# Dividing attention probabilities by their sums: in the transposing matmul instead of behind the values product

## The chip, the cores and the metric

The kernel runs on one core of a Trainium2 chip. TensorE multiplies and transposes and writes to PSUM, whose 8 banks hold 512 f32 columns each. VectorE, ScalarE and GpSimd do the rest, and each engine takes its instructions in program order, waiting on counting semaphores. The metric is device time in microseconds, lower is better.

## The reference, cut to what matters

One layer: RMSNorm, a combined projection, latent attention (8 heads) beside a gated MLP, then a mixture of experts and a last norm. The attention is, for 1024 rows in blocks of 128 queries:

```
sc = (einsum('bqhd,bkhd->bhqk', qn_i, k_nope)
      + einsum('bqhr,bkr->bhqk', qr_i, k_rope)).astype(float32) * scale
mask = key_chunk[None, :] <= q_chunk[:, None]        # chunks of 64 rows
p = softmax(where(mask, sc, neg), axis=-1)
o = einsum('bhqk,bkhd->bqhd', p, v)
```

So p is the exponentials divided by their row sums, and o is p times v. All of it is float32.

## The kernel before, in words

The stages follow each other in one program: norm and transposes, latents, attention ("A"), the gated MLP's projections ("U"), the gates and output products, the router, the experts. The sets of instructions of each engine are written out by hand, in the order in which they run. To keep float32 accuracy most products are done in three: each operand is split into a high part (`_hi`) and a rest (`_lo`), both of type fp32r, and `mm3` (L369 to L371) multiplies high by high, high by rest and rest by high. Transposes (`pe.transpose` with `ident`) and a few small products use plain f32.

Attention runs over 64 steps s, which are 8 heads h of 8 query blocks i. Block i sees i + 1 key tiles of 128. For each step:

- `scores(s)` on TensorE fills two PSUM banks with 128 queries by up to 1024 keys; `row_max(s)` on VectorE (L1274) takes the negative row maxima; `exponent(s)` on ScalarE (L987) writes the exponentials to `prob` and their row sums to `lsum`.
- `prob_transposes(s)` on TensorE (L658) turns each 128x128 tile of `prob`, four to a PSUM bank, in a pass; passes alternate between banks 4 and 5. ScalarE copies a pass to `pt_hi` (L1013) and VectorE takes the rest `pt_lo` (L1319).
- `values(s)` multiplies v by the turned tiles into bank 6, as 64 rows of one head by 128 queries. After four steps bank 6 is full, and ScalarE copies it to `o_t` (L979).

The row sums are taken care of once in four steps: `inverse_sums` on VectorE (L1280) makes four columns of reciprocals `rl`, `spread_sums` on TensorE (L667) turns each column, broadcast to 128 columns, so that bank 4 or 5 holds the reciprocal of each query in every partition, and `outputs` on VectorE (L1289) multiplies `o_t` by it. `PASSES` and `bank_of` give the spreads a place among the passes over banks 4 and 5.

TensorE's order in step s is `scores(s + 2)`, `prob_transposes(s)`, `values(s - 1)`, after every fourth step `spread_sums`, and in the first four steps of a head one `job` of the next head, which projects its queries or keys. VectorE's order is `row_max(s + 2)`, `pt_lo` of step s, `outputs`, `job_read`. ScalarE's is `exponent(s + 1)`, `pt_hi` of step s, `outputs`, `job_high`. `scores(s + 2)` waits until `exponent(s)` has read the banks that it fills.

Two plain f32 products that are no transposes stand outside attention: L574 multiplies squares by a column of ones, and L582 multiplies ones by the diagonal matrices `z_diag`. `link` makes VectorE wait for its own last instruction.

Of the kernel before, what the change touches and what calls it, by code (L numbers as in the profile page):

```python
# [20 lines left out]
F32 = mybir.dt.float32  # L21
# [4 lines left out]
ALU = mybir.AluOpType  # L26
ACT = mybir.ActivationFunctionType
AX = mybir.AxisListType.X

P = 128  # L30
# [4 lines left out]
HALF = 512  # L35
EPS = 1e-6
HEADS, NOPE, ROPE, VH = 8, 64, 32, 64
# [22 lines left out]
NQ = 64  # L60
# [17 lines left out]
def chunks_through(s):  # L78

    return sum((i % NT) // 4 + 1 for i in range(s + 1))  # L80

PASSES = []
for _s in range(NQ):
    PASSES += [(0, _c) for _c in range(chunks_through(_s - 1) if _s else 0, chunks_through(_s))]
    if _s % 4 == 0 and _s:
        PASSES.append((1, _s // 4 - 1))
PASSES.append((1, NQ // 4 - 1))  # L90
PASS_OF = {_x: _n for _n, _x in enumerate(PASSES)}


def build(nc, a, out, stop_after=None):
    base = 16512

    with ExitStack() as ctx:
        def at(name, kb, shape, dt):
            return nc.alloc_sbuf_tensor_at(name, shape, dt, offset=base + int(kb * KB))
# [3 lines left out]
        def sem(name):  # L103
            if name not in sems:
                sems[name] = ctx.enter_context(nc.semaphore(name))
            return sems[name]
# [64 lines left out]
        pt_hi = [at(f"pt_hi{i}", (20, 24, 36, 40)[i], [P, 4, P], F32R) for i in range(4)]  # L171
        pt_lo = [at(f"pt_lo{i}", (22, 26, 38, 42)[i], [P, 4, P], F32R) for i in range(4)]
        q_tmp = at("q_tmp", 6, [P, HALF], F32)
        q_hi = [at(f"q_hi{i}", 136 + 8 * i, [P, T], F32R) for i in range(2)]
        q_lo = [at(f"q_lo{i}", 140 + 8 * i, [P, T], F32R) for i in range(2)]
        v_hi = [at(f"v_hi{i}", 152 + 4 * i, [P, NT, VH], F32R) for i in range(2)]
# [224 lines left out]
        def head_values(h):  # L401

            p = h // 2
            return v_f[p // 2][:, (p % 2) * (p // 2 + 1), :, (h % 2) * VH:(h % 2 + 1) * VH]

        def bank_of(kind, n):
            return 4 + PASS_OF[kind, n] % 2

        def v_tiles_after(jj):

# [129 lines left out]
        def _(pe):  # L540
# [55 lines left out]
            if "A" in on:  # L596
# [44 lines left out]
                            mm = pe.matmul(dst[:, m - CHUNK:m], mask_l[:, :], mask_r[:, :], start=False, stop=True)  # L641
                    mm.then_inc(sem("s_done"), 1)

                def bank_free(kind, n):

                    if PASS_OF[kind, n] >= 2:
                        was, m = PASSES[PASS_OF[kind, n] - 2]
                        pe.wait_ge(sem("o_ready" if was else "pt_lo_ready"), m + 1)

                def prob_transposes(s):  # L650

                    i = s % NT
                    c0 = chunks_through(s - 1) if s else 0
                    pe.wait_ge(sem("exp_done"), s + 1)
                    for c in range(i // 4 + 1):
                        bank_free(0, c0 + c)
                        for j in range(4 * c, min(4 * c + 4, i + 1)):
                            mm = pe.transpose(ps[:, bank_of(0, c0 + c), (j % 4) * P:(j % 4) * P + P],  # L658
                                              prob[s % 2][:, j * P:(j + 1) * P], ident[:, :])
                        mm.then_inc(sem("pt_done"), 1)  # L660

                def spread_sums(g):

                    pe.wait_ge(sem("rl_ready"), g + 1)
                    bank_free(1, g)
                    for i in range(4):
                        mm = pe.transpose(ps[:, bank_of(1, g), i * P:(i + 1) * P],  # L667
                                          rl[:, 4 * g + i:4 * g + i + 1].to_broadcast([P, P]), ident[:, :])
                    mm.then_inc(sem("sums_spread"), 1)

                def values(s):

                    h, i = divmod(s, NT)
                    c0 = chunks_through(s - 1) if s else 0
                    pe.wait_ge(sem("v_split"), h + 1)
                    pe.wait_ge(sem("pt_lo_ready"), chunks_through(s))
                    if s and s % 4 == 0:
                        pe.wait_ge(sem("o_copied"), s // 4)
                    dst = ps[0:VH, 6, (i % 4) * P:(i % 4 + 1) * P]
                    for j in range(i + 1):  # L680
                        c = (c0 + j // 4) % 4
                        mm = mm3(pe, dst, (v_hi[h % 2][:, j, :], v_lo[h % 2][:, j, :]),
                                 (pt_hi[c][:, j % 4, :], pt_lo[c][:, j % 4, :]), j == 0, j == i)
                    mm.then_inc(sem("pv_done"), 1)
# [17 lines left out]
                for s in range(NQ):  # L702
                    if s + 2 < NQ:
                        scores(s + 2)
                    prob_transposes(s)
                    if s:
                        values(s - 1)
                        if s % 4 == 0:
                            spread_sums(s // 4 - 1)
                    h, i = divmod(s, NT)  # L710
                    if i < 4 and h + 1 < HEADS:
                        job(h + 1, i)
                values(NQ - 1)
                spread_sums(NQ // 4 - 1)
            if "U" in on:
                def v_rows(t):

# [195 lines left out]
        def _(act):  # L913
# [50 lines left out]
            if "A" in on:  # L964
# [9 lines left out]
                def outputs(g):  # L974

                    h, c = divmod(g, 2)
                    r = (h % 2) * VH
                    act.wait_ge(sem("pv_done"), 4 * g + 4)
                    act.activation(o_t[r:r + VH, h // 2, c * HALF:(c + 1) * HALF], ps[0:VH, 6, :], ACT.Copy).then_inc(sem("o_copied"), 1)  # L979

                def exponent(s):
                    n = (s % NT + 1) * P
# [17 lines left out]
                for s in range(NQ):  # L1000
                    h, i = divmod(s, NT)
                    if s + 1 < NQ:
                        exponent(s + 1)
                    c0 = chunks_through(s - 1) if s else 0
                    for c in range(i // 4 + 1):
                        w = min(4, i + 1 - 4 * c)
                        cc = c0 + c
                        act.wait_ge(sem("pt_done"), cc + 1)
                        if cc >= 4:

                            used = next(x for x in range(s + 1) if chunks_through(x) > cc - 4)
                            act.wait_ge(sem("pv_done"), used + 1)
                        act.activation(pt_hi[cc % 4][:, 0:w, :].rearrange("p a b -> p (a b)"), ps[:, bank_of(0, cc), 0:w * P],  # L1013
                                       ACT.Copy).then_inc(sem("pt_hi_ready"), 1)
                    if s % 4 == 0 and s:
                        outputs(s // 4 - 1)
                    if i < 4 and h + 1 < HEADS:
                        job_high(h + 1, i)
# [136 lines left out]
        def _(dve):  # L1155
            steps = [0]

            def link(ins):

                steps[0] += 1  # L1160
                ins.then_inc(sem("dve_step"), 1)
                dve.wait_ge(sem("dve_step"), steps[0])
# [95 lines left out]
            if "A" in on:  # L1258
# [15 lines left out]
                    dve.tensor_reduce(negm[:, s:s + 1], ps[:, b:b + 2, :].rearrange("p b c -> p (b c)")[:, 0:n], AX, ALU.max,  # L1274
                                      negate=True).then_inc(sem("max_ready"), 1)

                def inverse_sums(g):

                    dve.wait_ge(sem("exp_done"), 4 * g + 4)
                    dve.reciprocal(rl[:, 4 * g:4 * g + 4], lsum[:, 4 * g:4 * g + 4]).then_inc(sem("rl_ready"), 1)  # L1280

                def outputs(g):

                    h, c = divmod(g, 2)
                    r = (h % 2) * VH
                    o = o_t[r:r + VH, h // 2, c * HALF:(c + 1) * HALF]
                    dve.wait_ge(sem("o_copied"), g + 1)
                    dve.wait_ge(sem("sums_spread"), g + 1)
                    dve.tensor_tensor(o, ps[r:r + VH, bank_of(1, g), :], o, ALU.mult).then_inc(sem("o_ready"), 1)  # L1289

                for t in range(1, NT, 2):
                    dve.wait_ge(sem("v_done"), t + 1)
# [12 lines left out]
                    job_read(0, j)  # L1305
                row_max(0)
                row_max(1)
                for s in range(NQ):
                    h, i = divmod(s, NT)
                    if (s + 1) % 4 == 3:  # L1310
                        inverse_sums((s + 1) // 4)
                    if s + 2 < NQ:
                        row_max(s + 2)
                    c0 = chunks_through(s - 1) if s else 0
                    for c in range(i // 4 + 1):
                        w = min(4, i + 1 - 4 * c)
                        cc = c0 + c
                        dve.wait_ge(sem("pt_hi_ready"), cc + 1)
                        dve.tensor_tensor(pt_lo[cc % 4][:, 0:w, :].rearrange("p a b -> p (a b)"), ps[:, bank_of(0, cc), 0:w * P],  # L1319
                                          pt_hi[cc % 4][:, 0:w, :].rearrange("p a b -> p (a b)").bitcast(F32), ALU.subtract).then_inc(sem("pt_lo_ready"), 1)  # L1320
                    if s % 4 == 0 and s:
                        outputs(s // 4 - 1)
                    if i < 4 and h + 1 < HEADS:
                        job_read(h + 1, i)
                outputs(NQ // 4 - 1)
            if "O" in on:
                for k in range(KS):
                    dve.wait_ge(sem("ot_hi_ready"), k + 1)
# [408 lines left out]
```

## Time and profile before

| | |
|---|---|
| median of 3 runs | 1250.52 us (1250.46 to 1253.19) |
| the profiled execution | 1250.46 us, of which span 1248.4 us |
| TensorE busy | 1108.9 us, 89% of the span |
| VectorE, ScalarE, GpSimd busy | 712.3, 564.8, 327.0 us |
| granted clock, mean | 0.951 |
| attention, `job` of the first head to the last `spread_sums` | about 97 to 300 us |

Each row of the profile names a line of the kernel, the engine, and output<-inputs. TensorE's weight loads are an engine of their own in it (PEld), beside the matmuls (PE). A matmul's end is modelled: the distance from one start to the next tells more than its duration. An idle time is put down to the engine that ended it.

### The profile page before, as it was taken

The page shows a single profiled execution, that of the slowest core. Times are in us where ns is not written, and L with a number is a line of the kernel's source. Part 1 is how long each engine was busy: PE and PEld are TensorE (multiplying, and loading weights), DVE is VectorE, ACT ScalarE, POOL GpSimd, SP SyncE. Part 2 cuts the span into 40 slices and gives each one's busy share as a digit, 9 for nine tenths or more (in the row PEclk, how much of TensorE's full clock was granted, in tenths as well). Part 3 has the DMA queues.
Part 4 walks back from the last instruction along what each step waited for, and adds up shares of the span by engine and source line. Part 5 has one row for each costly group of instructions (what it writes and reads, how often), then busy time and mean ns, then how long its engine had stood idle before and what let it go on. Part 6 is the DMA issues. An engine that isn't in the chain of part 4 may idle for free.

```text
span 1248.4 us, 18136 instructions
## 1 busy us (share of the span) xinstructions
PE 1108.9 (89%) x6835; PEld 963.9 (77%) x6835; DVE 712.3 (57%) x832; ACT 564.8 (45%) x756; POOL 327.0 (26%) x276
## 2 busy tenths in 40 slices
PE   3998999999999899999998999329999999999940
PEld 3885888888877788888887888329999999999930
DVE  5874666666055711111114232558888888888838
ACT  5334655655144200000003221407888888888823
POOL 3103222212332223333220000122444444444210
PEclk9988999999999999999999999659999999999975
DMA  7010000021204111111113322537999999999737
GB/s 244 1 28 11 7 7 7 7 69 34 52 1 111 34 34 51 49 37 50 51 51 104 105 75 77 212 121 300 394 368 356 341 348 356 363 379 358 284 141 288
DMA packets 93131, 184.27 MB, mean 148 GB/s; under 512 B 29712, under 2 KB 67088, under 8 KB 79248
## 3 DMA queue, kind: packets, MB, share of 16 engines
q1 hardware_dynamic: 82704, 166.65, 38.4%
q0 software_dynamic: 10368, 16.80, 3.6%
q8 instruction: 41, 0.67, 0.2%
q14 instruction: 18, 0.15, 0.0%
HBM read 177.12 MB, written 27.26 MB: 164 GB/s over the span
## 4 chain that ended last, share of the span: by engine, by line
PE 78%; DVE 11%; ACT 4%; issue 2%; DMA 2%; SPq 1%; POOL 0%; ACTq 0%; POOLq 0%; DVEq 0%
PE ps L369 24%; PE ps L371 23%; PE ps L370 23%; PE ps L858 3%; PE ps L658 2%; DVE pt_lo L1319 1%; PE ps L818 1%; DVE negm L1274 1%; SPq L348 1%; DVE q_tmp L1265 1%; ACT prob L987 1%; DVE acc L1600 1%; DVE res L1610 1%; DVE acc L1601 1%; PE ps L667 1%
## 5 line engine op out<-in xcount | busy, mean ns | idle before, releaser
L1554 DVE TENSOR_TENSOR we_lo<-raw_e,we_hi 128x2048 fp32r<-128x2048 f32 x108 | 246.9, 2288 | 48.3 <-ACT we_hi L1096 48.3
L1096 ACT ACTIVATE we_hi<-raw_e 128x2048 fp32r<-128x2048 f32 x108 | 206.1, 1908 | 8.3 <-DMA raw_e<-in_w_exp_gate_dram 3.7
L369 PE MATMUL ps<-ht_hi,w_hi 128*128 128x512 f32 x448 | 176.4, 394 | 0.4 <-DVE ht_lo L1192 0.4
L371 PE MATMUL ps<-ht_hi,w_lo 128*128 128x512 f32 x448 | 174.7, 390 | 0.0
L370 PE MATMUL ps<-ht_lo,w_hi 128*128 128x512 f32 x448 | 174.6, 390 | 0.0
L369 PE MATMUL ps<-we_hi,xst_hi 128*128 128x256 f32 x576 | 169.4, 294 | 0.0
L370 PE MATMUL ps<-we_lo,xst_hi 128*128 128x256 f32 x576 | 163.5, 284 | 0.0
L371 PE MATMUL ps<-we_hi,xst_lo 128*128 128x256 f32 x576 | 163.4, 284 | 0.0
L363 POOL CAST w_hi<-raw 128x1024 fp32r<-128x1024 f32 x36 | 40.7, 1130 | 302.2 <-PE ps L371 270.3
L369 PEld LDWEIGHTS ps<-we_hi,xst_hi 128*128 128x128 f32 x576 | 111.4, 193 | 0.0
L370 PEld LDWEIGHTS ps<-we_lo,xst_hi 128*128 128x128 f32 x576 | 111.1, 193 | 0.0
L371 PEld LDWEIGHTS ps<-we_hi,xst_lo 128*128 128x128 f32 x576 | 110.9, 193 | 0.0
L1398 DVE TENSOR_TENSOR mix<-ps,mix 128x512 f32<-128x512 f32 x16 | 11.1, 691 | 167.6 <-PE ps L371 167.6
L369 PEld LDWEIGHTS ps<-ht_hi,w_hi 128*128 128x128 f32 x448 | 84.4, 188 | 18.1 <-issue 1.0
L371 PEld LDWEIGHTS ps<-ht_hi,w_lo 128*128 128x128 f32 x448 | 84.2, 188 | 17.7
L370 PEld LDWEIGHTS ps<-ht_lo,w_hi 128*128 128x128 f32 x448 | 84.4, 188 | 17.3 <-issue 0.2
L364 POOL TENSOR_TENSOR w_lo<-raw,w_hi 128x1024 fp32r<-128x1024 f32 x36 | 87.4, 2428 | 2.9
L1053 ACT ACTIVATE mix<-ps 128x512 f32<-128x512 f32 x16 | 8.7, 598 | 146.4 <-PE ps L371 146.4
L1674 POOL COPY xcol<-xidx 128x1 uint32 (+1 forms) x36 | 61.5, 1709 | 36.6 <-DVE xidx L1548 34.6
L369 PE MATMUL ps<-we_hi,hidt_hi 128*128 128x512 f32 x144 | 59.5, 413 | 4.8 <-DVE hidt_lo L1568 2.5
L1319 DVE TENSOR_TENSOR pt_lo<-ps,pt_hi 128x512 fp32r<-128x512 f32 (+2 forms) x96 | 50.5, 553 | 20.9 <-ACT pt_hi L1013 20.6
L1013 ACT ACTIVATE pt_hi<-ps 128x512 fp32r<-128x512 f32 (+2 forms) x96 | 43.5, 488 | 36.8 <-PE ps L658 36.8
(284 smaller groups left out, 2472.8 us busy)
## 6 DMA issues: line engine op xcount, KB each, us to landing
raw_e<-in_w_exp_gate_dram SPq DMA_DIRECT2D x36, 1024.0 KB, 8.6
raw_e<-in_w_exp_up_dram SPq DMA_DIRECT2D x36, 1024.0 KB, 7.9
raw_e<-in_w_exp_down_dram SPq DMA_DIRECT2D x36, 1024.0 KB, 8.7
raw<-in_w_in_dram SPq DMA_DIRECT2D x27, 512.0 KB, 3.8
yin<-y_dram SPq DMA_DIRECT2D x16, 512.0 KB, 6.6
xin<-in_x_dram SPq DMA_DIRECT2D x8, 512.0 KB, 7.2
raw<-in_w_out_dram SPq DMA_DIRECT2D x8, 512.0 KB, 4.1
xre<-in_x_dram SPq DMA_DIRECT2D x8, 512.0 KB, 4.2
```

Source lines behind the costliest of these rows:

```text
L363: pool_link(pool, pool.tensor_copy(w_hi[n % 3][:, :, :], raw[n % 3][:, :, :]))
L364: pool.tensor_tensor(w_lo[n % 3][:, :, :], raw[n % 3][:, :, :], w_hi[n % 3][:, :, :].bitcast(F32), ALU.subtract).then_inc(sem("w_split"), 1)
L369: pe.matmul(dst, st[0], mv[0], start=first, stop=False)
L370: pe.matmul(dst, st[0], mv[1], start=False, stop=False)
L371: return pe.matmul(dst, st[1], mv[0], start=False, stop=last)
L658: mm = pe.transpose(ps[:, bank_of(0, c0 + c), (j % 4) * P:(j % 4) * P + P], prob[s % 2][:, j * P:(j + 1) * P], ident[:, :])
L858: mm = pe.transpose(ps[:, k // 4, (k % 4) * P:(k % 4) * P + P], v[:, k, :], ident[:, :])
L1013: act.activation(pt_hi[cc % 4][:, 0:w, :].rearrange("p a b -> p (a b)"), ps[:, bank_of(0, cc), 0:w * P], ACT.Copy).then_inc(sem("pt_hi_rea ...
L1096: act.activation(we_hi[c % 4][:, :], raw_e[c % 6][:, :], ACT.Copy).then_inc(sem("w_hi_ready"), 1)
L1319: dve.tensor_tensor(pt_lo[cc % 4][:, 0:w, :].rearrange("p a b -> p (a b)"), ps[:, bank_of(0, cc), 0:w * P], pt_hi[cc % 4][:, 0:w, :].rearr ...
L1554: dve.tensor_tensor(we_lo[c % 4][:, :], raw_e[c % 6][:, :], we_hi[c % 4][:, :].bitcast(F32), ALU.subtract).then_inc(sem("w_lo_ready"), 1)
L1674: pool.tensor_copy(xcol[j % 4][:, :], xidx[:, column(it, j)]).then_inc(sem("xcol_ready"), 1)
```

## The change

The division moves from behind the values product into the transposing. On VectorE `diagonal(s)` takes the reciprocal of one column of row sums and multiplies the identity by it, to a 128x128 f32 tile `rl_diag` (two buffers). `prob_transposes(s)` multiplies each tile of `prob` by `rl_diag` in a plain f32 matmul where it transposed it with the identity, so that `pt_hi` and `pt_lo` hold probabilities that are already divided. It waits for `diag_ready` instead of `exp_done`. `inverse_sums`, `spread_sums` and VectorE's `outputs` go away, and with them the list of passes: banks 4 and 5 alternate over the chunks alone. ScalarE's copy to `o_t` is the last step.

```
-                    pe.wait_ge(sem("exp_done"), s + 1)
+                    pe.wait_ge(sem("diag_ready"), s + 1)
                     for c in range(i // 4 + 1):
-                        bank_free(0, c0 + c)
+                        if c0 + c >= 2:
+                            pe.wait_ge(sem("pt_lo_ready"), c0 + c - 1)
                         for j in range(4 * c, min(4 * c + 4, i + 1)):
-                            mm = pe.transpose(ps[:, bank_of(0, c0 + c), (j % 4) * P:(j % 4) * P + P],
-                                              prob[s % 2][:, j * P:(j + 1) * P], ident[:, :])
+                            mm = pe.matmul(ps[:, 4 + (c0 + c) % 2, (j % 4) * P:(j % 4) * P + P],
+                                           prob[s % 2][:, j * P:(j + 1) * P], rl_diag[s % 2][:, :], start=True, stop=True)
                         mm.then_inc(sem("pt_done"), 1)
-                def spread_sums(g):
...
-                        if s % 4 == 0:
-                            spread_sums(s // 4 - 1)
...
-                def inverse_sums(g):
...
-                def outputs(g):
...
-                    dve.tensor_tensor(o, ps[r:r + VH, bank_of(1, g), :], o, ALU.mult).then_inc(sem("o_ready"), 1)
+                def diagonal(s):
+
+                    dve.wait_ge(sem("exp_done"), s + 1)
+                    link(dve.reciprocal(rl[:, s:s + 1], lsum[:, s:s + 1]))
+                    if s >= 2:
+                        dve.wait_ge(sem("pt_done"), chunks_through(s - 2))
+                    dve.tensor_scalar(rl_diag[s % 2][:, :], ident[:, :], rl[:, s:s + 1], None, ALU.mult).then_inc(sem("diag_ready"), 1)
...
                 row_max(0)
                 row_max(1)
+                diagonal(0)
                 for s in range(NQ):
                     h, i = divmod(s, NT)
-                    if (s + 1) % 4 == 3:
-                        inverse_sums((s + 1) // 4)
+                    if s + 1 < NQ:
+                        diagonal(s + 1)
                     if s + 2 < NQ:
                         row_max(s + 2)
```

On TensorE, at the eighth block of the first head, before: scores with their mask (L641), then eight transposes with `ident`, then the values product.

```order
L369 MATMUL ps<-k_hi_141,q_hi_132 128x256
L370 MATMUL ps<-k_lo_143,q_hi_132 128x256
L371 MATMUL ps<-k_hi_141,q_lo_134 128x256
L641 MATMUL ps<-mask_r,mask_l 128x64
L658 MATMUL ps<-ident,prob_145 128x128 x8
L369 MATMUL ps<-pt_hi_122,v_hi_135 64x128
L370 MATMUL ps<-pt_lo_126,v_hi_135 64x128
```

The same place in the changed program, whose lines are numbered 10 to 18 lower:

```order
L359 MATMUL ps<-k_hi_143,q_hi_134 128x256
L360 MATMUL ps<-k_lo_145,q_hi_134 128x256
L361 MATMUL ps<-k_hi_143,q_lo_136 128x256
L628 MATMUL ps<-mask_r,mask_l 128x64
L640 MATMUL ps<-rl_diag_132,prob_147 128x128 x8
L359 MATMUL ps<-pt_hi_122,v_hi_137 64x128
L360 MATMUL ps<-pt_lo_126,v_hi_137 64x128
```

Only the operand has changed from `ident` to `rl_diag`, and the kind of the instruction from a transpose to a matmul.

On TensorE after the values product of the eighth block, before: four broadcast columns are turned (L667), then the next head's projection (`c_hi`, `h_hi`) starts.

```order
L369 MATMUL ps<-pt_hi_125,v_hi_135 64x128
L370 MATMUL ps<-pt_lo_129,v_hi_135 64x128
L371 MATMUL ps<-pt_hi_125,v_lo_137 64x128
L667 MATMUL ps<-ident,rl 128x128 x4
L369 MATMUL ps<-c_hi,h_hi_113 128x512
L370 MATMUL ps<-c_lo,h_hi_113 128x512
```

The same place in the changed program:

```order
L359 MATMUL ps<-pt_hi_125,v_hi_137 64x128
L360 MATMUL ps<-pt_lo_129,v_hi_137 64x128
L361 MATMUL ps<-pt_hi_125,v_lo_139 64x128
L359 MATMUL ps<-c_hi,h_hi_113 128x512
L360 MATMUL ps<-c_lo,h_hi_113 128x512
```

The turned columns are gone and nothing stands in their place.

On VectorE over the last three steps of the first head, before: `negm` is a row maximum, `pt_lo` the rest of a pass.

```order
L1274 TENSOR_REDUCE negm<-ps 128x1
L1319 TENSOR_TENSOR pt_lo_128<-ps,pt_hi_124 128x512
L1319 TENSOR_TENSOR pt_lo_129<-ps,pt_hi_125 128x256
L1280 RECIPROCAL rl<-lsum 128x4
L1274 TENSOR_REDUCE negm<-ps 128x1
L1319 TENSOR_TENSOR pt_lo_126<-ps,pt_hi_122 128x512
L1319 TENSOR_TENSOR pt_lo_127<-ps,pt_hi_123 128x384
L1274 TENSOR_REDUCE negm<-ps 128x1
L1319 TENSOR_TENSOR pt_lo_128<-ps,pt_hi_124 128x512
L1319 TENSOR_TENSOR pt_lo_129<-ps,pt_hi_125 128x512
```

The same steps in the changed program:

```order
L1250 RECIPROCAL rl<-lsum 128x1
L1253 TENSOR_SCALAR rl_diag_132<-ident,rl 128x128
L1244 TENSOR_REDUCE negm<-ps 128x1
L1284 TENSOR_TENSOR pt_lo_126<-ps,pt_hi_122 128x512
L1284 TENSOR_TENSOR pt_lo_127<-ps,pt_hi_123 128x384
L1250 RECIPROCAL rl<-lsum 128x1
L1253 TENSOR_SCALAR rl_diag_131<-ident,rl 128x128
L1244 TENSOR_REDUCE negm<-ps 128x1
L1284 TENSOR_TENSOR pt_lo_128<-ps,pt_hi_124 128x512
L1284 TENSOR_TENSOR pt_lo_129<-ps,pt_hi_125 128x512
L1250 RECIPROCAL rl<-lsum 128x1
L1253 TENSOR_SCALAR rl_diag_132<-ident,rl 128x128
```

A reciprocal of one column and a 128x128 product now stand ahead of each row maximum, behind the `pt_lo` of the step before.

## Rows read from the trace of the kernel before

**Rows 1.** The page: busy time and share; granted TensorE clock in 40 slices.
```profile
PE 1108.9 (89%) x6835; PEld 963.9 (77%) x6835; DVE 712.3 (57%) x832; ACT 564.8 (45%) x756; POOL 327.0 (26%) x276
...
PEclk9988999999999999999999999659999999999975
```

**Rows 2.** Busy time by engine: a middle head, and the last one.
```profile
184.30:208.80 24.50, 23.33 (x216) 20.28 (x215) 16.36 (x28) 14.65 (x34) 5.76 (x7) 1.00 0.04 8
...
282.00:301.00 19.00, 17.27 (x181) 15.67 (x180) 11.72 (x20) 11.17 (x23) 0.81 (x1) 1.00 0.01 2
```

**Rows 3.** TensorE groups, whole run: count, busy us, mean ns, idle before.
```profile
L658 PE MATMUL ps<-ident,prob 128*128 128x128 f32 x288 | 44.2, 280 | 1.3 <-DVE pt_lo L1319 1.0
...
L667 PE MATMUL ps<-ident,rl 128*128 128x128 f32 x64 | 9.9, 277 | 5.4 <-DVE pt_lo L1319 5.4
...
L574 PE MATMUL ps<-ones,c_sq 128*128 128x1 f32 x48 | 5.8, 254 | 0.0
...
L582 PE MATMUL ps<-z_diag,ones 128*128 128x512 f32 x8 | 4.2, 642 | 0.0
```

**Rows 4.** TensorE in order of time: start, us, line, shapes, count, idle before.
```profile
186.78 0.47 PE L369 MATMUL ps<-k_hi,q_hi 128*128 128x512 f32 x1 [0.31 <-ACT prob L987]
...
196.22 0.62 PE L667 MATMUL ps<-ident,rl 128*128 128x128 f32 x4 [0.68 <-DVE pt_lo L1319]
196.60 0.48 PE L369 MATMUL ps<-k_hi,q_hi 128*128 128x512 f32 x1
...
200.04 0.20 PE L641 MATMUL ps<-mask_r,mask_l 128*128 128x64 bf16 x1
200.42 0.96 PE L658 MATMUL ps<-ident,prob 128*128 128x128 f32 x7 [0.17 <-DVE pt_lo L1319]
...
202.73 1.07 PE L658 MATMUL ps<-ident,prob 128*128 128x128 f32 x8
203.56 0.30 PE L369 MATMUL ps<-pt_hi,v_hi 128*64 128x128 f32 x1
```

**Rows 5.** The same view where 128x512 f32 matmuls stand among split ones.
```profile
68.51 0.39 PE L371 MATMUL ps<-ht_hi,w_lo 128*128 128x512 f32 x1
68.74 1.88 PE L582 MATMUL ps<-z_diag,ones 128*128 128x512 f32 x4
...
70.68 0.40 PE L370 MATMUL ps<-ht_lo,w_hi 128*128 128x512 f32 x1
```

**Rows 6.** The same view where the 128x1 f32 matmuls stand.
```profile
56.01 1.84 PE L574 MATMUL ps<-ones,c_sq 128*128 128x1 f32 x16
...
58.03 0.40 PE L370 MATMUL ps<-ht_lo,w_hi 128*128 128x512 f32 x1
```

**Rows 7.** Weight loads of the four broadcasts: count, busy, mean, idle before.
```profile
L667 PEld LDWEIGHTS ps<-ident,rl 128*128 128x128 f32 x64 | 6.6, 136 | 6.3 <-issue 6.3
```

**Rows 8.** ScalarE early in a head, ahead of the fifth score block.
```profile
185.45 0.63 ACT L970 ACTIVATE q_hi<-q_tmp 128x512 fp32r<-128x512 f32 x1 [2.03 <-DVE q_tmp L1265]
...
185.99 0.56 ACT L987 ACTIVATE prob<-ps,negm 128x384 f32<-128x384 f32 x1
```

**Rows 9.** VectorE groups, whole run: reciprocals, scalar operation, the removed product.
```profile
L1289 DVE TENSOR_TENSOR o_t<-ps,o_t 64x512 f32<-64x512 f32 x16 | 11.0, 688 | 18.0 <-ACT o_t L979 12.6 <-PE ps L667 5.4
...
L1280 DVE RECIPROCAL rl<-lsum 128x4 f32<-128x4 f32 x16 | 2.8, 172 | 2.7 <-ACT prob L987 2.7
...
L1426 DVE RECIPROCAL rstd<-std 128x1 f32<-128x1 f32 x8 | 1.3, 164 | 13.6 <-ACT std L1082 13.6
...
L1165 DVE TENSOR_SCALAR ident<-iota_row,iota_col 128x128 f32<-128x128 f32 x1 | 0.3, 288 | 1.2 <-POOL iota_col L1618 1.2
```

**Rows 10.** VectorE groups in the attention stage, 95 to 301 us: the row maxima.
```profile
L1274 DVE TENSOR_REDUCE negm<-ps 128x1 f32<-128x128 f32 (+3 forms) x64 | 47.8, 748 | 14.7 <-PE ps L641 14.0
```

**Rows 11.** ScalarE groups there: exponentials and the reads of their sums.
```profile
L987 ACT ACTIVATE prob<-ps,negm 128x128 f32<-128x128 f32 (+3 forms) x64 | 47.0, 735 | 0.3
...
L987 ACT ACTIVATION_READ_ACCUMULATOR prob<-ps,negm 128x1 f32 x64 | 12.6, 198 | 0.0
```

More of the change, by code:

```diff
@@ L80, in chunks_through @@
     return sum((i % NT) // 4 + 1 for i in range(s + 1))
[L85 to L91, printed above, removed]
 def build(nc, a, out, stop_after=None):
@@ L173, in build @@
         q_tmp = at("q_tmp", 6, [P, HALF], F32)
+        rl_diag = [at(f"rl_diag{i}", 5 + i / 2, [P, P], F32) for i in range(2)]
         q_hi = [at(f"q_hi{i}", 136 + 8 * i, [P, T], F32R) for i in range(2)]
@@ L404, in head_values @@
             return v_f[p // 2][:, (p % 2) * (p // 2 + 1), :, (h % 2) * VH:(h % 2 + 1) * VH]
-        def bank_of(kind, n):
-            return 4 + PASS_OF[kind, n] % 2
         def v_tiles_after(jj):
@@ L642, in scores @@
                     mm.then_inc(sem("s_done"), 1)
[L644 to L648, printed above, removed]
                 def prob_transposes(s):
@@ L653, in prob_transposes @@
                     c0 = chunks_through(s - 1) if s else 0
-                    pe.wait_ge(sem("exp_done"), s + 1)
+                    pe.wait_ge(sem("diag_ready"), s + 1)
                     for c in range(i // 4 + 1):
-                        bank_free(0, c0 + c)
+                        if c0 + c >= 2:
+                            pe.wait_ge(sem("pt_lo_ready"), c0 + c - 1)
                         for j in range(4 * c, min(4 * c + 4, i + 1)):
-                            mm = pe.transpose(ps[:, bank_of(0, c0 + c), (j % 4) * P:(j % 4) * P + P],
-                                              prob[s % 2][:, j * P:(j + 1) * P], ident[:, :])
+                            mm = pe.matmul(ps[:, 4 + (c0 + c) % 2, (j % 4) * P:(j % 4) * P + P],
+                                           prob[s % 2][:, j * P:(j + 1) * P], rl_diag[s % 2][:, :], start=True, stop=True)
                         mm.then_inc(sem("pt_done"), 1)
-                def spread_sums(g):
[L664 to L669, printed above, removed]
                 def values(s):
@@ L677, in values @@
                     if s and s % 4 == 0:
-                        pe.wait_ge(sem("o_copied"), s // 4)
+                        pe.wait_ge(sem("o_ready"), s // 4)
                     dst = ps[0:VH, 6, (i % 4) * P:(i % 4 + 1) * P]
@@ L713, in _ @@
                 values(NQ - 1)
-                spread_sums(NQ // 4 - 1)
             if "U" in on:
@@ L978, in outputs @@
                     act.wait_ge(sem("pv_done"), 4 * g + 4)
-                    act.activation(o_t[r:r + VH, h // 2, c * HALF:(c + 1) * HALF], ps[0:VH, 6, :], ACT.Copy).then_inc(sem("o_copied"), 1)
+                    act.activation(o_t[r:r + VH, h // 2, c * HALF:(c + 1) * HALF], ps[0:VH, 6, :], ACT.Copy).then_inc(sem("o_ready"), 1)
                 def exponent(s):
@@ L1012, in _ @@
                             act.wait_ge(sem("pv_done"), used + 1)
-                        act.activation(pt_hi[cc % 4][:, 0:w, :].rearrange("p a b -> p (a b)"), ps[:, bank_of(0, cc), 0:w * P],
+                        act.activation(pt_hi[cc % 4][:, 0:w, :].rearrange("p a b -> p (a b)"), ps[:, 4 + cc % 2, 0:w * P],
                                        ACT.Copy).then_inc(sem("pt_hi_ready"), 1)
@@ L1275, in row_max @@
                                       negate=True).then_inc(sem("max_ready"), 1)
-                def inverse_sums(g):
-                    dve.wait_ge(sem("exp_done"), 4 * g + 4)
-                    dve.reciprocal(rl[:, 4 * g:4 * g + 4], lsum[:, 4 * g:4 * g + 4]).then_inc(sem("rl_ready"), 1)
-                def outputs(g):
[L1284 to L1288, printed above, removed]
-                    dve.tensor_tensor(o, ps[r:r + VH, bank_of(1, g), :], o, ALU.mult).then_inc(sem("o_ready"), 1)
+                def diagonal(s):
[4 more added lines that the diff above has]
+                    dve.tensor_scalar(rl_diag[s % 2][:, :], ident[:, :], rl[:, s:s + 1], None, ALU.mult).then_inc(sem("diag_ready"), 1)
                 for t in range(1, NT, 2):
@@ L1318, in _ @@
                         dve.wait_ge(sem("pt_hi_ready"), cc + 1)
-                        dve.tensor_tensor(pt_lo[cc % 4][:, 0:w, :].rearrange("p a b -> p (a b)"), ps[:, bank_of(0, cc), 0:w * P],
+                        dve.tensor_tensor(pt_lo[cc % 4][:, 0:w, :].rearrange("p a b -> p (a b)"), ps[:, 4 + cc % 2, 0:w * P],
                                           pt_hi[cc % 4][:, 0:w, :].rearrange("p a b -> p (a b)").bitcast(F32), ALU.subtract).then_inc(sem("pt_lo_ready"), 1)
-                    if s % 4 == 0 and s:
-                        outputs(s // 4 - 1)
                     if i < 4 and h + 1 < HEADS:
                         job_read(h + 1, i)
-                outputs(NQ // 4 - 1)
             if "O" in on:
```

## The prediction

> **What bounds the kernel now.** I read the page's first two parts first. TensorE is busy for 1108.9 us of the span of 1248.4 us, and its granted clock is at nine tenths or full in all slices but the first ones and two stretches far behind attention [rows 1]. The change touches attention alone, so the next view is the busy time in stretches. In a middle head of 24.5 us TensorE is busy for 23.33 us at the full clock (2.4 GHz), VectorE for 16.36 us and ScalarE for 14.65 us. The last head, which has no projections beside it, has TensorE busy for 17.27 of 19.0 us [rows 2]. TensorE's work sets the pace of a head, and the other two can only put holes into it. TensorE in order of time shows the holes: one before the fifth score block, where it waits for an exponential (idle 0.31 us), one before the turned sums (0.68 us), a small one before the seventh block's transposes (0.17 us) [rows 4]. So what the change does to TensorE's own time comes first, and what it does to these holes second.
>
> **The transposes become matmuls: the large term.** There are 288 of them, 36 tiles in each of 8 heads [rows 3]. Eight stand from 202.73 to 203.56 us, where the values product starts, which is 0.104 us for one [rows 4]; I take 0.107. What a plain f32 matmul of 128 columns takes, no row of attention shows. Two others do. L582 has 4 matmuls in the program (two in each of two calls) and 8 records in the trace; L574 has 24 and 48 records [rows 3]. One plain f32 matmul is two records, one transpose is one. Four records of L582, 512 columns each, stand between 68.74 us and the split product behind them. Split products of 512 columns start 0.23 us apart (68.51 to 68.74), so that the first one behind them started in effect at 70.68 - 0.23 = 70.45 us. That is 1.71 / 4 = 0.427 us for a record, and a quarter of it, 0.107 us, for 128 columns, if columns set it [rows 5]. L574 has one column, so that its records show the loading of weights alone: (58.03 - 0.23 - 56.01) / 16 = 0.112 us for a record [rows 6]. At 128 columns load and columns are about equal. Where they overlap, as under L582, a matmul costs 2 x 0.107 to 2 x 0.112 us, and the transpose before it 0.107. I take 0.11 us more for a tile: 288 x 0.11 = +31.7 us. The bounds: 288 x 0.107 = 30.8 and 288 x 0.117 = 33.7 where they overlap; nothing added if a record of this shape held all of it (against the two counts of rows 3); and if load and columns ran one after the other, 2 x (0.107 + 0.107) = 0.428 us, which is +0.321 us for a tile and +92.4 us in all. The nearest rows are the two of 0.107 and 0.112, and I stay with them.
>
> The Trainium skill, page "TensorE: Matmul & The Clock Gate", section Terms, calls trn2's transpose mode 4 times faster for FP32. If that held for a tile here, a matmul would take four times 0.107 us, and the time would come out as in the second rival below. The trace disagrees as far as it goes: two records of 0.107 us make a factor of two.
>
> **The turned sums go.** There were 16 groups of four. One takes 196.60 - 196.22 = 0.38 us [rows 4], so -6.1 us, all of it on TensorE's path. The wait in front of the groups goes with them. It comes in every second group, because the four columns need the bank whose last `pt_lo` VectorE has just finished: 5.4 us by the matmul rows [rows 3], 6.3 us by the rows of the weight loads, which don't have modelled ends [rows 7]. The score block or projection behind it needs nothing that is so late, so I count -6.3 us. VectorE also loses 16 products of 0.688 us and 16 reciprocals of 0.172 us, 13.8 us [rows 9]. They are not on the path and I cost them at nothing.
>
> **The diagonals on VectorE.** The nearest rows are a reciprocal of one column (0.164 us) and the building of the identity, 128x128 f32 with one scalar operand (0.288 us) [rows 9]. With a hop of 0.03 us between them a diagonal is 0.48 us, and 64 of them are 30.8 us. VectorE's load in a middle head goes from 16.36 to about 18.5 us (+3.9, -1.7), in a head that will last near 27. As work this is hidden. As order it isn't free. `diagonal(s + 1)` waits for the exponential of step s + 1, and `row_max(s + 2)`, the `pt_lo` of step s and `job_read` are queued behind it. Before, `row_max(s + 2)` waited only for its scores. The exponential after it, and TensorE two steps on, wait for that maximum.
>
> I followed one head through by these durations. Three places matter. At the second block the exponential of the third (185.99 us) stands behind `q_hi` on ScalarE [rows 8], and TensorE waits for it with its fifth score block [rows 4]. That chain starts at the projection in the first block, and the two tiles of the second block stand on TensorE between this projection and the hole, so their 2 x 0.11 us fall into it: 0.2 us in 7 heads, -1.5 us. At the third block the row maximum of the fourth now starts only after that exponential and its diagonal, about 1.8 us later than before, `pt_lo` and `k_lo` follow it, and the next projection waits for `k_lo` by about 0.15 us. At the seventh block the transposes wait for the `pt_lo` of the sixth, which now stands behind the diagonal as well as the long row maximum: the step from 200.04 to 200.42 us grows by about 0.1 us. With some more for what I can't follow, 0.3 us in each of 8 heads, +2.4 us. The bounds: -7 us, if the longer matmuls hide the rest of the holes (1.17 us of idle TensorE in a middle head [rows 2], less the 0.68 already counted and what stays for the projection chain, doubled for the seams that the rows don't count as idle), and +12 us as in the first rival.
>
> **The rest.** Passes over banks 4 and 5 now alternate without the sums between them. The wait that this leaves is for a `pt_lo` two passes back, as before. ScalarE's copy to `o_t` stays as it was. The end of attention has its last turned group removed, which is in the 16. The stages behind it start from TensorE's end of attention and only shift. Attention runs at full clock, so nothing is to be gained there. The cold stretch at its start contains one tile.
>
> **The sum.** 31.7 - 6.1 - 6.3 - 1.5 + 2.4 = +20.2 us. On the profiled execution, 1250.46 us (a span of 1248.4 and 2.1 around it), that is 1270.7 us. The median of the three runs, 1250.52, is the same within 0.1 us.
>
> **Rivals.**
> 1. VectorE and ScalarE become a second bound. Row maximum, exponential, reading of the sum and diagonal now form a chain from step to step. Over attention that is 47.8 [rows 10] + 47.0 + 12.6 [rows 11] + 30.8, and hops of about 0.15 us in each of 64 steps, 9.6: 148 us against some 225 us of attention. So it doesn't bind as a whole. Over the first blocks of a head, where TensorE's step is 2 us and `job_read` stands in the same queue, it can. If 1.5 us a head stay instead of 0.3, that is +9.6 us: 1280. Chance 0.14.
> 2. The load and the columns of a plain f32 matmul do not overlap at 128 columns, where both are equally long. +92.4 - 6.1 - 6.3 and all new waits hidden: +80 us, 1330. For it speaks that no row has this shape; against it that under L582 the loads are hidden to the last 0.01 us. Chance 0.03.
> 3. The other side. A plain matmul by a diagonal of this shape costs TensorE no more than the transpose. Then -6.1 - 6.3 + 2.4 = -10 us, 1240.5. It decides from the point where a tile costs less than 10 / 288 = 0.035 us more. Against it stand both counts of records and both distances. Chance 0.03.
> 4. The longer matmuls swallow the holes, the -7 us of above with the added tile at 0.107: 30.8 - 6.1 - 6.3 - 7 = +11.4 us, 1262. I count this as the low end of the forecast.
>
> **How the numbers follow.** Forecast with its end in 4: 0.80, rivals 1 to 3: 0.14, 0.03, 0.03. The likeliest runs from 1262 to 1276. To hold 8 in 10 with the first rival, the range is 1262 to 1281. A change under 0.3% (3.75 us) can't be told from none; only values between the third rival and the forecast would fall there. Faster 0.03, same 0.02, slower 0.95.
>
> **What would show it.** In the changed profile the matmuls by `rl_diag` come as 576 records, and eight of them take 1.7 us from the first start to the values product; 288 records or 0.85 us would be rival 3, 3.4 us rival 2. TensorE shows no wait of 0.68 us after the fourth block. A middle head lasts about 27.0 us. VectorE's diagonal takes 0.16 + 0.29 us. TensorE's wait at the seventh block is a little longer. If TensorE is idle for over 2 us a head, waiting for diagonals, exponentials or `pt_lo`, rival 1 holds. I am wrong if stages behind attention change in length.

## The result and the profile after

| | before | changed |
|---|---|---|
| median | 1251.86 us (4 runs, 1250.46 to 1255.22) | 1272.65 us (4 runs, 1270.96 to 1276.1) |
| profiled execution, its span | 1250.46, 1248.4 us | 1271.58, 1269.4 us |
| attention, second projection of the first head to the next stage's first product | 97.74 to 300.33, 202.6 us | 93.25 to 317.26, 224.0 us |
| a middle head | 24.43 us | 26.89 us |

The ratio is 1.0162, 95% interval 1.0133 to 1.0191: slower by 1.6%, and the forecast was 1270.7 us. The attention stage alone is 21.4 us longer. The stages ahead of it are 4.5 us shorter and those behind it 4.1 us longer (948.1 and 952.1 us). That isn't the change's doing: in twelve profiles of kernels that differ only in attention, attention began between 93.2 and 97.7 us and the stages behind it took 948 to 954 us, and 948.5 in the one where the changed kernel has only two VectorE steps in another order. The prediction had named a change behind attention as a sign of being wrong; 4.1 us lie within that spread, so they don't serve as one. So I compare attention, and in it the middle head, which repeats to 0.15 us in most runs and to 0.3 us in the worst: the mean distance between the eighth blocks' first transposes (or matmuls) over heads 3 to 7.

The page of the changed kernel, parts 1 and 2, beside [rows 1]:

```profile
PE 1137.7 (90%) x7059; PEld 993.0 (78%) x7059; DVE 725.4 (57%) x928; ACT 567.4 (45%) x756; POOL 327.4 (26%) x276
...
PEclk7998999999999989999999999759999999999975
```
TensorE has 28.8 us more to do and 224 more records: 288 come with the second record of each tile, 64 go with the sums. A middle head of the changed kernel, beside [rows 2] (span, then busy time of TensorE, weight loads, VectorE, ScalarE, GpSimd, clock, DMA):

```profile
209.55:236.40 26.85, 26.83 (x246) 23.88 (x244) 17.81 (x41) 14.88 (x34) 5.76 (x6) 1.00 0.04 8
```
TensorE is busy without a hole. VectorE is at 17.81 us. The group that replaces L658 of [rows 3], over the whole run:

```profile
L640 PE MATMUL ps<-rl_diag,prob 128*128 128x128 f32 x576 | 80.2, 285 | 1.1 <-DVE rl_diag L1253 0.8 <-DVE pt_lo L1284 0.3
```
576 records for 288 tiles. TensorE in order of time, pieces beside [rows 4]:

```profile
182.58 2.03 PE L640 MATMUL ps<-rl_diag,prob 128*128 128x128 f32 x16
184.36 0.30 PE L359 MATMUL ps<-pt_hi,v_hi 128*64 128x128 f32 x1
...
191.82 0.47 PE L359 MATMUL ps<-k_hi,q_hi 128*128 128x512 f32 x1
...
193.97 0.22 PE L361 MATMUL ps<-pt_hi,v_lo 128*64 128x128 f32 x1
194.15 0.50 PE L359 MATMUL ps<-c_hi,h_hi 128*128 128x512 f32 x1
...
202.02 0.22 PE L361 MATMUL ps<-pt_hi,v_lo 128*64 128x128 f32 x1
202.08 0.45 PE L359 MATMUL ps<-k_hi,q_hi 128*128 128x512 f32 x1
...
206.21 0.20 PE L628 MATMUL ps<-mask_r,mask_l 128*128 128x64 bf16 x1
206.39 1.80 PE L640 MATMUL ps<-rl_diag,prob 128*128 128x128 f32 x14
```
Eight tiles take 184.36 - 182.58 = 1.78 us where they took 0.83. The fifth score block (191.82) shows no wait any more. After the fourth block's values (202.02) the next scores follow at once (202.08): the wait of 0.68 us in front of the sums is gone with them. The projection of the third block starts 0.18 us after the last product (193.97 to 194.15) instead of 0.06: the late `k_lo`. The seventh block's matmuls start 0.18 us after the mask (206.21 to 206.39), less than the 0.38 us of before.

The diagonals, beside [rows 9]; line, shapes, count, busy us, mean ns:

```profile
L1253 DVE TENSOR_SCALAR rl_diag<-ident,rl 128x128 f32<-128x128 f32 x64 | 23.3, 364 | 2.5 <-DVE rl L1250 0.3
...
L1250 DVE RECIPROCAL rl<-lsum 128x1 f32<-128x1 f32 x64 | 10.1, 158 | 34.6 <-ACT prob L957 34.6
```
A reciprocal takes 0.158 us, most products 0.287 us. The mean of 0.364 comes from 14 that take longer, one of them 1.88 us.

### The profile page after: what moved, and what is told of

Its sections match the earlier page's. It is cut to its first block, busy times and chain, and to the rows that moved or that the text cites. A ratio compares the mean times of both kernels' runs of the same rounds, so it can differ in the third digit from the quotient of the medians.

```text
span 1269.4 us, 18710 instructions
## 1 busy us (share of the span) xinstructions
PE 1137.7 (90%) x7059; PEld 993.0 (78%) x7059; DVE 725.4 (57%) x928; ACT 567.4 (45%) x756; POOL 327.4 (26%) x276
## 4 chain that ended last, share of the span: by engine, by line
PE 83%; DVE 9%; ACT 3%; DMA 2%; issue 2%; SPq 1%; POOL 0%; POOLq 0%; DVEq 0%; ACTq 0%
PE ps L359 24%; PE ps L361 23%; PE ps L360 23%; PE ps L640 5%; PE ps L828 3%; PE ps L788 1%; SPq L338 1%; DVE acc L1562 1%; DVE res L1572 1%; DVE acc L1563 1%; DMA xs<-h_dram,xcol 1%; PE ps L848 1%; PE ps L777 1%; DVE st_f L1311 1%; DVE we_lo L1516 1%
## 5 line engine op out<-in xcount | busy, mean ns | idle before, releaser
L640 PE MATMUL ps<-rl_diag,prob 128*128 128x128 f32 x576 | 80.2, 285 | 1.1 <-DVE rl_diag L1253 0.8
L640 PEld LDWEIGHTS ps<-rl_diag,prob 128*128 128x128 f32 x576 | 70.2, 193 | 1.5 <-DVE rl_diag L1253 0.9
```

The costliest lines, as they stand in the source:

```text
L640: mm = pe.matmul(ps[:, 4 + (c0 + c) % 2, (j % 4) * P:(j % 4) * P + P], prob[s % 2][:, j * P:(j + 1) * P], rl_diag[s % 2][:, :], start=True ...
```

## The experiments

Middle heads, and ratios of times to the kernel before on the same chip:

| run | middle head, us | ratio to before | interval |
|---|---|---|---|
| before | 24.43 | | |
| changed | 26.89 | 1.0162 | 1.0133 to 1.0191 |
| plain matmul alone | 28.22 | 1.0255 | 1.0229 to 1.0282 |
| no division | 22.75 | 0.9888 | 0.9863 to 0.9914 |
| diagonals alone | 24.36 | 1.0014 | 0.9997 to 1.0032 |
| plain matmul, no division | 26.70 | 1.0140 | 1.0102 to 1.0177 |
| diagonals alone, maximum first | 23.14 | 0.9934 | 0.9905 to 0.9963 |
| changed, maximum first | 26.68 | 1.0156 | 1.0126 to 1.0186 |
| changed, split elsewhere | 26.94 | 1.0161 | 1.0134 to 1.0188 |
| changed, three mends | 26.43 | 1.0141 | 1.0108 to 1.0175 |
| before, sums in bank 7 | 23.59 | 0.9965 | 0.9951 to 0.9979 |
| the same, late query | 23.00 | 0.9930 | 0.9908 to 0.9952 |

**The matmul alone, in the kernel before.**

```
-  mm = pe.transpose(ps[...], prob[s % 2][:, j * P:(j + 1) * P], ident[:, :])
+  mm = pe.matmul(ps[...], prob[s % 2][:, j * P:(j + 1) * P], ident[:, :], start=True, stop=True)
```

> The kernel before with one thing changed: the 288 tiles of prob are turned by a plain f32 matmul with the identity instead of a transpose. Sums, spreads and the product by them stay. Theory (TensorE's own time): 576 records, eight tiles take 1.77 us instead of 0.83, 0.11 us more for a tile is 3.96 us in a head, of which 0.2 fall into the hole before the fifth score block, so a middle head lasts 28.1 to 28.4 us (24.45 before) and the whole takes 28 to 31 us more, near 1280 us: more than the whole change (+21). Rival (the change is slow mostly for its diagonals and their waits): a middle head under 26.5 us, the whole under +15 us.

A middle head of 28.22 us and a median of 1281.16 us beside 1250.29: as the theory says. The instruction alone costs more than the change as a whole.

**No division at all.** The changed kernel with transposes by the identity, waiting for `exp_done`, and without `diagonal`.

> Transposes with the identity as before, and no division at all: no reciprocals, no turned sums, no product on VectorE, no diagonals. The attention output is left undivided. Theory: what the change takes away is worth 0.38 us for each of 16 groups and 6.3 us of waits in front of 8 of them, so a middle head lasts 22.9 us and the whole takes 12.4 us less than before, 1239 us. Rival (the waits come back at the next consumer of bank or pt_lo): a middle head of 23.6 us or more, 6 us less at most.

The median is 1236.67 us beside 1250.29, attention 12.3 us shorter than before (190.3 us), the middle head 22.75 us. In attention, what the change takes away is worth what the forecast said, 12.4 us. One head, the longest of the middle ones (span, then busy times as above):

```profile
195.98:218.82 22.84, 22.50 (x209) 19.33 (x208) 14.55 (x25) 14.40 (x34) 5.75 (x6) 1.00 0.05 9
```
**Diagonals beside transposes.** As the changed kernel, but

```
-  mm = pe.matmul(..., prob[...], rl_diag[s % 2][:, :], start=True, stop=True)
+  mm = pe.transpose(..., prob[...], ident[:, :])
```

> The changed kernel with the diagonals made and waited for as in the change, but the tiles turned with the identity by a transpose; so the division is left out. Beside the run without division it shows what the diagonals and their place in VectorE's order cost while TensorE has 0.11 us a tile less to hide them. Theory: 0.3 us a head when hidden by the longer matmuls, up to 0.8 us here: a middle head of 23.2 to 23.7 us, 2 to 6 us more than without division. Rival (row maximum, exponential and diagonal form the bound): a middle head above 24.4 us, 12 us or more above the run without division.

1.62 us a head over no division, 12.6 us in attention (202.9 us) and 15.6 us between the medians. The theory allowed 0.8 us at most and was wrong; the head is at the rival's edge of 24.4, and the whole is beyond its 12 us. One head, the longest of the middle ones, and TensorE's waits from 150 to 285 us (for whom, total, times, longest):

```profile
201.63:226.21 24.58, 23.21 (x209) 19.44 (x208) 17.52 (x41) 14.61 (x34) 5.72 (x6) 1.00 0.04 9
```
```profile
PE ps L640 <- DVE pt_lo L1284: 4.0, 6, 0.7
PE ps L359 <- ACT prob L957: 1.4, 5, 0.3
PE ps L359 <- DVE pt_lo L1284: 1.0, 5, 0.2
```
VectorE is busy for 17.5 of 24.6 us: it isn't full. TensorE waits for `pt_lo`, which it hardly did without diagonals. VectorE's and ScalarE's order shows why, here at a head's third block:

```profile
209.13 1.28 POOL L1609 TENSOR_TENSOR q_lo<-q_tmp,q_hi 128x512 fp32r<-128x512 f32 x1 [0.92 <-ACT q_hi L940]
...
209.65 0.16 DVE L1250 RECIPROCAL rl<-lsum 128x1 f32<-128x1 f32 x1 [1.32 <-ACT prob L957]
...
209.85 0.65 DVE L1253 TENSOR_SCALAR rl_diag<-ident,rl 128x128 f32<-128x128 f32 x1
...
210.41 0.68 DVE L1244 TENSOR_REDUCE negm<-ps 128x1 f32<-128x512 f32 x1
...
211.13 0.69 ACT L957 ACTIVATE prob<-ps,negm 128x512 f32<-128x512 f32 x1 [0.77 <-DVE negm L1244]
```
The row maximum at 210.41 stands behind a reciprocal and a diagonal, which wait for an exponential that ended its sum at 209.6. Its scores were done before 208.4, so it starts 2 us late. Most of that, 1.3 us, is VectorE's wait for the exponential; some of it is that the product takes 0.65 us here where most take 0.287: it ends with GpSimd's `q_lo` (209.13 + 1.28 = 210.41; more of this with GpSimd's split below). The next exponential (211.13, idle 0.77 us before it) waits for that maximum.

**The matmul without division.** The run without division, with the first experiment's edit.

> The run without division, with the tiles turned by a plain f32 matmul with the identity: the changed kernel without its diagonals and without their place in VectorE's order. The division is left out. Theory (the diagonals cost 0.3 us a head beside the longer matmuls, 1.6 us beside transposes): a middle head of 26.5 to 26.7 us, which is 22.74 and 3.8, and 0.2 to 0.4 us less than the changed kernel's 26.89. Rival (the diagonals cost 1.6 us a head in the change too): a middle head of 25.3 us.

26.70 us, 3.95 us a head over transposes, and attention 220.4 us instead of 190.3.

```profile
210.09:236.79 26.70, 26.68 (x246) 23.81 (x244) 15.06 (x24) 14.74 (x34) 5.76 (x6) 1.00 0.04 8
```
TensorE is full. The changed kernel's diagonals add 0.19 us to this, where they add 1.62 us beside transposes: the matmuls hide the rest. At the seventh block the matmuls follow the mask at once, where the changed kernel's start 0.18 us after it:

```profile
206.88 0.20 PE L628 MATMUL ps<-mask_r,mask_l 128*128 128x64 bf16 x1
206.92 1.81 PE L640 MATMUL ps<-ident,prob 128*128 128x128 f32 x14
```

**The maximum first**, beside transposes and in the changed kernel:

```
-  if s + 1 < NQ: diagonal(s + 1)
   if s + 2 < NQ: row_max(s + 2)
+  if s + 1 < NQ: diagonal(s + 1)
```

> Diagonals made and waited for beside transposes (division left out), with row_max(s + 2) ahead of diagonal(s + 1). Theory (what the diagonals cost is their place ahead of the row maximum, and what is late is k_lo of the projection and pt_lo): the middle head goes from 24.36 to 22.9 to 23.4 us. Rival (the transposes wait for the diagonals themselves, or VectorE's added work is what counts): it stays at 24.0 us or above.

> The changed kernel with row_max(s + 2) ahead of diagonal(s + 1) on VectorE. Theory: the late row maximum of the fourth block and the k_lo behind it go, and the wait at the seventh block shrinks: 0.2 to 0.3 us a head, a middle head of 26.6 instead of 26.9 us, 2 us less in all, which the time can hardly show and the profile can. Rival (the transposing matmuls now wait for diagonals that stand behind long row maxima): a middle head over 27.2 us.

Both as the theory says: 24.36 to 23.14 us beside transposes, 26.89 to 26.68 us in the change. The same instructions on VectorE cost 0.4 instead of 1.6 us a head when they stand one place later. The same third block beside transposes, now with the maximum first:

```profile
204.90 0.69 DVE L1244 TENSOR_REDUCE negm<-ps 128x1 f32<-128x512 f32 x1
206.17 0.17 DVE L1250 RECIPROCAL rl<-lsum 128x1 f32<-128x1 f32 x1 [0.58 <-ACT prob L957]
206.37 0.65 DVE L1253 TENSOR_SCALAR rl_diag<-ident,rl 128x128 f32<-128x128 f32 x1
```
The product is as long as before (0.65 us), but the maximum no longer stands behind it. In the change the gain can't be told by the time, only by the profile.

**GpSimd's split elsewhere.** In the changed kernel's profile the product of 1.88 us stands beside a GpSimd instruction:

```profile
136.24 2.37 POOL L354 TENSOR_TENSOR w_lo<-raw,w_hi 128x1024 fp32r<-128x1024 f32 x1
...
136.81 1.88 DVE L1253 TENSOR_SCALAR rl_diag<-ident,rl 128x128 f32<-128x128 f32 x1
...
138.75 0.74 PEld L640 LDWEIGHTS ps<-rl_diag,prob 128*128 128x128 f32 x6 [0.87 <-DVE rl_diag L1253]
```
GpSimd's `w_lo` ends at 136.24 + 2.37 = 138.61, the product at 138.69, and TensorE waits for it (0.76 us). The second head lasts 28.26 us.

```
-  if h == 1 and "U" in on: split_units(pool, NZ, NZ + 1)     # behind value_split(h + 1)
+  if h == 2 and "U" in on: split_units(pool, NZ, NZ + 1)     # ahead of head_split(h + 1)
```

> The changed kernel, with GpSimd's split of the first weight unit of the next stage (2.4 us) moved behind the third head's query parts, so that it falls into the second half of the second head. In the changed profile one diagonal takes 1.88 us instead of 0.29 and ends with that split; the second head lasts 28.3 us against 26.9 for the others. Theory (VectorE's product and GpSimd hold the same path to SBUF by turns): no diagonal of 1.9 us that TensorE waits for remains, the second head lasts 26.9 to 27.2 us, 1 us less in all. Rival (something else about the second head): it stays at 28.3 us.

The second head's distance is 27.27 us: 1.0 us less, but just outside the 26.9 to 27.2 us expected. A product is stretched again beside the split's new place, to the same end (148.06 + 2.38 = 150.44, and 149.35 + 1.17 = 150.52). TensorE doesn't wait for that product itself, but the row maximum and the `pt_lo` behind it are late, and the sixth block's matmuls wait for that `pt_lo`. They start 0.34 us later than in the run without diagonals, which is what the second head still has over the others:

```profile
148.06 2.38 POOL L354 TENSOR_TENSOR w_lo<-raw,w_hi 128x1024 fp32r<-128x1024 f32 x1
...
149.35 1.17 DVE L1253 TENSOR_SCALAR rl_diag<-ident,rl 128x128 f32<-128x128 f32 x1
150.44 1.08 DVE L1244 TENSOR_REDUCE negm<-ps 128x1 f32<-128x896 f32 x1
151.44 0.87 DVE L1284 TENSOR_TENSOR pt_lo<-ps,pt_hi 128x512 fp32r<-128x512 f32 x2
...
152.27 0.91 PE L640 MATMUL ps<-rl_diag,prob 128*128 128x128 f32 x6 [0.17 <-DVE pt_lo L1284]
```

**All three mends together:** the maximum first, the split elsewhere, and ScalarE's `q_hi` behind the next exponential.

> The changed kernel, complete, with three mends: row_max(s + 2) ahead of the diagonal, GpSimd's weight split in the second half of the second head, ScalarE's q_hi behind the next exponential. Theory (TensorE's own time remains): the hole before the fifth score block goes, a middle head of 26.3 to 26.5 us and the second head no longer than 26.9, 4 to 5 us less than the changed kernel, 1267 us, still 17 us above the kernel before. Rival: once nothing waits, the change comes within 10 us of before.

26.43 us, the second head too, median 1268.78 beside 1250.63. From 150 to 285 us the profile shows no wait of TensorE's matmuls any more, and the change is still 1.4% slower than before.

**The sums in bank 7, in the kernel before.**

```
-  return 4 + PASS_OF[kind, n] % 2
+  return 7 if kind and n % 2 == 0 else 4 + PASS_OF[kind, n] % 2
```

Even groups leave the list of passes and wait for the last `k_lo` of the head's projections; `job(h, 0)` waits for `o_ready` of the group that used bank 7 two heads back.

> The kernel before, with the turned sums of blocks 0 to 3 of each head put into bank 7, which the projections have left by then, instead of bank 4 or 5. Everything is computed as before. Theory: the hole of 0.68 us (0.84 us from the last product's start) comes from the bank alone, so it goes: a middle head of 23.7 to 23.8 us, 5 to 6 us less in all, 1245 us. Rival (TensorE waits for the same pt_lo one instruction later): a middle head of 24.3 us or more, no gain that can be told.

0.84 us a head, attention 6.7 us shorter (195.9 us), median 1245.69 us beside 1249.96, ratio 0.9965. The theory holds, with a little more in attention and a little less in the whole than it said. The turned sums (L671 here) follow the last product without a hole:

```profile
213.77 0.22 PE L371 MATMUL ps<-pt_hi,v_lo 128*64 128x128 f32 x1
213.83 0.62 PE L671 MATMUL ps<-ident,rl 128*128 128x128 f32 x4
214.20 0.48 PE L369 MATMUL ps<-k_hi,q_hi 128*128 128x512 f32 x1
```
**And the query's high part behind the exponential.**

```
   exponent(s + 1)
+  if i in (1, 3) and h + 1 < HEADS: job_high(h + 1, i - 1)
...
-  if i < 4 and h + 1 < HEADS: job_high(h + 1, i)
+  if i in (1, 3) and h + 1 < HEADS: job_high(h + 1, i)
```

> The kernel with the sums of blocks 0 to 3 in bank 7, and besides ScalarE's q_hi of a projection set behind the next exponential instead of ahead of it. Everything is computed as before. Theory: the hole before the fifth score block (0.31 us idle, 0.5 us from start to start) is q_hi ahead of the exponential, and goes too: a middle head of 23.2 to 23.4 us, 3 us less than with bank 7 alone, about 1242 us. Rival (that exponential waits for its row maximum, or GpSimd's q_lo gets late): the same as with bank 7 alone, or slower.

23.00 us a head, slightly better than expected, median 1240.06 us beside 1249.96, ratio 0.993 with 1 outside its interval. This version beats both kernels. ScalarE, then TensorE at the fifth score block:

```profile
200.25 0.58 ACT L991 ACTIVATE prob<-ps,negm 128x384 f32<-128x384 f32 x1
...
202.26 0.63 ACT L974 ACTIVATE q_hi<-q_tmp 128x512 fp32r<-128x512 f32 x1 [1.34 <-DVE q_tmp L1271]
```
```profile
202.90 0.39 PE L371 MATMUL ps<-c_hi,h_lo 128*64 128x512 f32 x1
203.12 0.39 PE L369 MATMUL ps<-k_hi,q_hi 128*128 128x512 f32 x1
```
The exponential of the third block (200.25) runs ahead of `q_hi` (202.26), and the fifth score block (203.12) starts 0.22 us after the last projection product.

## Why the prediction was right, step by step

- **One tile costs 0.11 us more.** Right in kind, small in size. Two records it is. From the first start to the values product the eight groups of a head take 8.04 us together instead of 3.55 (the two runs without division): 0.125 us for a tile, 35.9 us in all. That is outside the bound of 33.7. From one size of group to the next a transposed tile adds 0.109 us and a matmul tile 0.222, 0.114 more, and each group gained about 0.05 us besides, which the forecast had at nothing (a group of one tile went from 0.06 to 0.22).
- **Two tiles fall into the hole at the fifth score block.** Right, but it was not all: of 4.49 us a middle head 0.54 are hidden, 0.27 us there (the second block's step is 2.68 us in both runs), 0.21 us at the seventh block, where the transposes waited for a bank, and the rest in small pieces. I had put 0.2. The two errors cancel: attention is 30.1 us longer between the two runs without division, against 31.7 - 1.5 = 30.2. That the forecast comes so near is therefore partly luck: each of the two terms was off by over 4 us.
- **The turned sums and the wait before them.** -6.1 - 6.3 against 12.3 us less attention measured. That the wait belongs to the bank is shown by the sums in bank 7, where it is gone with everything else in place: 0.84 us a head, 8 heads, 6.7 us.
- **The diagonals cost 0.3 us a head.** In a middle head 0.19 us. Of this 0.14 is at the third block, near the 0.15 of the forecast: the projection waits for the late `k_lo` (0.09), and the values product for a late `pt_lo` (0.05). The rest is at the seventh block, which starts 0.13 us later than without diagonals, in every second head alone; I had put 0.1 in each. At the third block the product is held by GpSimd too (0.66 us instead of 0.287), which I had not counted. The second head pays 1.4 us more than the others; 1.0 of it goes when the split is moved, and the other 0.34 is the split's hold again, in its new place. In all 3.6 us instead of 2.4 (224.0 less 220.4).
- **The first rival** (VectorE and ScalarE as a second bound) is false for the change but nearer than I had it. With transposes the diagonals alone take back what the change saves: 1.68 us a head saved, 1.62 lost. My argument, that the chain's 148 us are far from 225, spoke of sums; the cost comes from one place in a queue, and the runs with the maximum first show it to be the place and not the load.
- **The second and third rivals** are excluded by 1.78 us for eight tiles: 2.1 times the transposes' 0.83. The Trainium skill, page "TensorE: Matmul & The Clock Gate", section Terms, has transposing 4 times faster for FP32. At this size the trace shows a factor of two.
- **The fourth** (the longer matmuls swallow the holes, counted as the low end) is half true: attention hides 5.8 us of the matmuls (35.9 less 30.1), but a tile costs more than the 0.107 us that it was added up with.

Attention loses 30.1 us by the matmuls and 3.6 by the diagonals to win 12.3: the 21.4 us measured. The change moves a division from 16 groups of four small transposes and 16 products into 288 matmuls that existed as transposes and cost half as much.

## What to carry to other kernels

A transpose is not free room for a multiplication in plain f32: count the records of a plain f32 matmul elsewhere in the trace before folding anything into one. A new instruction on a helper engine is priced by what stands behind it in that queue; set it behind whatever the bottleneck asks for next. And where a small step shows a wait, ask which buffer it waits for: here, in the kernel before, another PSUM bank and one exchanged pair of instructions on ScalarE were worth 0.7%, and moving the division cost 1.6%.

## What the runs showed of the hardware that I had not expected

VectorE's 128x128 product from SBUF to SBUF with one scalar operand takes 0.287 us alone and is held while GpSimd subtracts: 14 of 64 took 0.44 to 1.88 us, and each of the 14 ended 0.08 us after a GpSimd subtraction that had begun before it. VectorE's maxima and `pt_lo`, which read PSUM, show no such stretching: at one size their times differ by 0.02 us at most. The Trainium skill, page "SBUF — State Buffer", section Who interferes with whom, counts `tensor_scalar`, which this product is, among the operations that can run in a mode with two ports. In such a mode VectorE and GpSimd take an exclusive lock on the ports that they share, and the later one blocks until the other ends. The trace agrees (1.88 us against 0.287); which mode the product ran in no run here shows. I had priced the diagonal by the identity's row alone, and the rule would have told me to ask what GpSimd does at that time.
